# Strips of weights in passes, weight splits moved ahead, and level blocks in two alternating halves, in a two-layer hybrid block on one core

## The chip, the cores and the metric

The kernel runs on one core of one Trainium2 chip. The metric is the device time of one execution in microseconds. Three runs of the kernel before gave a median of 2342.08 us, from 2341.09 to 2344.77. The profile and the trace come from one further execution of 2344.89 us, whose span from the first to the last instruction is 2343.1 us.

## The reference

Two transformer-like blocks are applied to 512 positions (16 meta tokens are put in front, so there are 528 rows of width 1024). Everything is float32. The first block projects its normed input to retention, differential attention, a short convolution and three gates, sums the gated branches and ends with a squared-relu feed-forward. The second one has stick-breaking attention, gated linear attention (GLA) and a gated feed-forward with a convolution. What matters here, cut down:

```python
# block one
h = rms_norm(x, norm1_w)
(rq, rk, rv, rg, dq, dk, dv, cb, cc, cx, gates) = [h @ w_in[:, s:e] for s, e in column_bounds()]
ret = head_layer_norm(retention(rq, rk, rv)) * silu(rg)
diff = diff_attention(dq, dk, dv, lam, subln_w, lam_init)     # lam from four short vectors (diff_lambda)
conv = cb * short_conv(cc * cx, conv_w)
g = sigmoid(gates)
x = x + (g0 * (ret @ wb0) + g1 * (diff @ wb1) + g2 * (conv @ wb2)) @ w_out
x = x + square(relu(rms_norm(x, norm2_w) @ w_up)) @ w_down
# block two
sb = stick_breaking(q, k, v)
o = rmsnorm(gla(gq, gk, gv, glog)) * silu(g_r)                # causal, with a decay for each key channel
h = h + rmsnorm((gate_sb * (sb @ w_sb_out) + gate_gla * (o @ w_gla_out)) @ w_o)
h = h + rmsnorm((gelu(conv(hn @ w_ffn_up)) * (hn @ w_ffn_gate)) @ w_ffn_down)
```

## The kernel before

Every product with a weight matrix is cut into **strips**: 128 output columns, over up to eight chunks (`KC`) of 128 input rows. There are 338 strips, numbered through in the order of `PHASES`; two slots, even and odd numbers, hold their weights and results. To keep float32 precision, weights and inputs are split into a high and a low part, and a strip is the sum of high by high, high weight by low input, and low weight by high input. The stations of a strip:

- SyncE loads the raw weights into `wraw` (`load`), 512 KB. It waits for `lo_done` of the strip two before.
- ScalarE makes `wh` (`split_hi`, L355), when the weights have landed and the strip two before is multiplied (`mm_done`), and counts `hi_done`.
- VectorE makes `wl = wraw - wh` (`split_lo`, L857), when `hi_done` says so, and counts `lo_done`.
- TensorE multiplies (`strip`, L1548), then counts `mm_done`. The inputs are `xh`, `xl` or `bh`, `bl`. A strip over all 528 rows (T) is 48 matmuls of 264 columns, a strip over 512 positions (SEQ) is 24 of 512 columns. It waits at its start for `lo_done` of its own number and for the eviction of its slot, and with `ready` also chunk by chunk for its inputs. One chunk's three products (in steps: a step is one product of one chunk) come before the next chunk's.
- VectorE reads the result out of PSUM, mostly with the root of the norm as a factor (`scaled_by_root`, L890), and counts `evicted`.

Each engine's program is written out by hand, so the order in the code is the order in which an engine issues. `begin` (VectorE) is a `split_lo` of the next strip and a wait for the end of this one.

The **start**: ScalarE issues three small transfers (L384 to L386: `cst`, identity and ones; `col`, all columns of parameters; `lamr`, the four vectors for lambda), waits for the latter two (`params_in`, 32), and makes `xh` chunk by chunk (L363), with the `wh` of strip 0 behind the second. Behind the last come `wh` of strip 1 and the squares of x (L398). VectorE forms the lambda sums (L901), the low parts of x (L877), `wl` of strips 0 and 1, and adds up the squares (L883). TensorE sums over partitions in the middle of strip 1 (`first_sums`, L1615), and ScalarE takes the root (L379, L381). Strips 0, 1 and 2 are the first group of `conv_in`: `cc`, `cx` and `cb`; strip 2 uses slot 0.

**`gates_out`** (ScalarE) with `branch_out` (VectorE) and `branch_strips` (TensorE): for each of eight tiles a strip of gates, p0, and a strip of the branch's output matrix, p1; p2 is the next p0. The stage `sb_out` is of this kind with T-wide gates and only four chunks in p1.

**GLA** (L1933 and following): 32 iterations i, in each of which one strip is computed beside the attention of one chunk of 128 positions. `level_blocks` computes the attention inside the chunk as 64 by 64 blocks for two halves of 64 positions; each half has six levels and one diagonal product. The halves write to PSUM partitions 0 to 63 and 64 to 127 of the same bank.

## Time and profile before

| what | value |
|---|---|
| three runs | 2341.09, 2344.77, 2342.08 us (median 2342.08) |
| the profiled execution, its time | 2344.89 us |
| its span | 2343.1 us |
| TensorE busy with matmuls | 2271.0 us (97%), 13290 matmuls |
| VectorE, ScalarE, GpSimd busy | 1147.2, 780.6, 49.6 us |
| mean granted TensorE clock | 0.982 of full speed |

"Busy" counts running instructions only; waits, branches and DMA issues are not in it. Matmuls overlap, so the duration of one matmul is longer than its distance to the next; the starts of the rows are the better measure of the pace. "idle before <- releaser" in a row is how long the engine had stood still when the row began, and whose result ended that. A row that ends in x4 merges four like instructions and spans from the start of the first to the end of the last. PEclk 0.50 is the lower of the two levels of TensorE's clock, 1.2 GHz; 1.00 is 2.4 GHz.

### The profile page before, as it was taken

The page shows a single profiled execution, that of the slowest core. Times are in us where ns is not written, and L with a number is a line of the kernel's source. Part 1 is how long each engine was busy: PE and PEld are TensorE (multiplying, and loading weights), DVE is VectorE, ACT ScalarE, POOL GpSimd, SP SyncE. Part 2 cuts the span into 40 slices and gives each one's busy share as a digit, 9 for nine tenths or more (in the row PEclk, how much of TensorE's full clock was granted, in tenths as well). Part 3 has the DMA queues.
Part 4 walks back from the last instruction along what each step waited for, and adds up shares of the span by engine and source line. Part 5 has one row for each costly group of instructions (what it writes and reads, how often), then busy time and mean ns, then how long its engine had stood idle before and what let it go on. Part 6 is the DMA issues. An engine that isn't in the chain of part 4 may idle for free.

```text
span 2343.1 us, 34196 instructions
## 1 busy us (share of the span) xinstructions
PE 2271.0 (97%) x13290; PEld 1902.6 (81%) x13290; DVE 1147.2 (49%) x1726; ACT 780.6 (33%) x1207; POOL 49.6 (2%) x75
## 2 busy tenths in 40 slices
PE   7999999999999999999999999999999999999996
PEld 6988994777888788888888944789999998889895
DVE  5553322544555455454456322236765546646465
ACT  3222221322454444232234254324333324223222
POOL 0000000000000000000000000002210000000000
PEclk9999999999999999999999977999999999999999
DMA  3232220232222222222222300131113221222222
GB/s 126 90 107 90 90 81 10 72 108 81 73 68 69 101 98 95 99 91 90 100 91 88 126 1 0 63 136 64 55 55 147 90 90 64 94 94 91 99 90 99
DMA packets 53758, 197.69 MB, mean 84 GB/s; under 512 B 6928, under 2 KB 7312, under 8 KB 53024
## 3 DMA queue, kind: packets, MB, share of 16 engines
q1 hardware_dynamic: 49248, 179.39, 22.3%
q10 hardware_dynamic: 3456, 13.72, 1.6%
q0 software_dynamic: 960, 3.24, 0.5%
q8 instruction: 68, 1.11, 0.2%
q14 instruction: 26, 0.21, 0.0%
HBM read 189.91 MB, written 6.42 MB: 84 GB/s over the span
## 4 chain that ended last, share of the span: by engine, by line
PE 94%; DVE 3%; ACT 2%; issue 1%; DMA 0%; ACTq 0%; DVEq 0%
PE ps L1548 79%; PE ps L1805 1%; PE ps L1851 1%; PE ps L1930 1%; PE ps L1827 1%; PE ps L1716 1%; PE ps L1675 1%; PE ps L1744 1%; PE ps L1841 1%; DVE wl L857 1%; PE ps L1660 1%; ACT wh L355 1%; PE ps L1811 1%; PE ps L1848 0%; PE ps L1908 0%
## 5 line engine op out<-in xcount | busy, mean ns | idle before, releaser
L1548 PE MATMUL ps<-xh,wh 128*128 128x264 f32 (+1 forms) x2192 | 623.0, 333 | 28.2 <-DVE wl L857 20.3
L1548 PE MATMUL ps<-xl,wh 128*128 128x264 f32 (+1 forms) x2192 | 618.1, 331 | 0.0
L1548 PE MATMUL ps<-xh,wl 128*128 128x264 f32 (+1 forms) x2192 | 616.0, 330 | 0.0
L355 ACT ACTIVATE wh<-wraw 128x1024 fp32r<-128x1024 f32 x338 | 356.5, 1055 | 757.5 <-PE ps L1548 755.5
L857 DVE TENSOR_TENSOR wl<-wraw,wh 128x1024 fp32r<-128x1024 f32 x338 | 413.4, 1223 | 106.8 <-ACT wh L355 99.4
L1548 PE MATMUL ps<-bh,wh 128*128 128x264 f32 (+1 forms) x1600 | 448.0, 330 | 14.8 <-DVE wl L857 10.2
L1548 PE MATMUL ps<-bl,wh 128*128 128x264 f32 (+1 forms) x1600 | 445.6, 328 | 0.0
L1548 PE MATMUL ps<-bh,wl 128*128 128x264 f32 (+1 forms) x1600 | 444.2, 327 | 0.0
L1548 PEld LDWEIGHTS ps<-xh,wh 128*128 128x128 f32 x2192 | 373.5, 189 | 75.9 <-issue 19.6
L1548 PEld LDWEIGHTS ps<-xh,wl 128*128 128x128 f32 x2192 | 371.1, 190 | 37.9
L1548 PEld LDWEIGHTS ps<-xl,wh 128*128 128x128 f32 x2192 | 371.2, 189 | 37.1 <-issue 0.5
L1548 PEld LDWEIGHTS ps<-bh,wh 128*128 128x128 f32 x1600 | 268.7, 188 | 50.3 <-issue 12.6
L1548 PEld LDWEIGHTS ps<-bh,wl 128*128 128x128 f32 x1600 | 268.6, 188 | 26.7
L1548 PEld LDWEIGHTS ps<-bl,wh 128*128 128x128 f32 x1600 | 268.4, 188 | 26.7 <-issue 0.2
L890 DVE TENSOR_TENSOR gate<-ps,rsq 128x528 f32<-128x528 f32 (+1 forms) x32 | 22.4, 699 | 95.8 <-PE ps L1548 95.8
L890 DVE TENSOR_TENSOR tmp<-ps,rsq 128x528 f32<-128x528 f32 x34 | 24.1, 708 | 88.4 <-PE ps L1548 84.3
L890 DVE TENSOR_TENSOR qq<-ps,rsq 128x528 f32<-128x528 f32 (+2 forms) x36 | 25.3, 704 | 85.7 <-PE ps L1548 85.6
L363 ACT ACTIVATE bh<-hf 128x512 f32 (+1 forms) x38 | 24.0, 633 | 108.4 <-DVE hf L1495 53.7
L428 ACT ACTIVATE gate<-gate 128x512 f32<-128x512 f32 (+1 forms) x24 | 15.3, 637 | 132.2 <-DVE gate L890 132.2
L1201 DVE TENSOR_TENSOR res<-ps,res 128x512 f32 x24 | 16.6, 691 | 72.6 <-PE ps L1548 72.6
L1271 DVE SCALAR_TENSOR_TENSOR res<-ps,res 128x512 f32<-128x512 f32 (+3 forms) x32 | 17.8, 615 | 63.8 <-ACT res L666 63.8
L1218 DVE SCALAR_TENSOR_TENSOR hf<-ps,tmp 128x512 f32<-128x512 f32 x32 | 22.1, 691 | 46.0 <-ACT tmp L615 46.0
(349 smaller groups left out, 1797.8 us busy)
## 6 DMA issues: line engine op xcount, KB each, us to landing
wraw<-weights_dram SPq DMA_DIRECT2D x338, 512.0 KB, 3.2
hf<-tables_dram POOLq DMA_DIRECT2D x12, 264.0 KB, 3.0
res<-x_t_dram SPq DMA_DIRECT2D x4, 528.0 KB, 7.4
res<-x_t_dram ACTq DMA_DIRECT2D x1, 2112.0 KB, 10.6
res_dram<-res ACTq DMA_DIRECT2D x1, 2112.0 KB, 7.4
mrg_dram<-mrg ACTq DMA_DIRECT2D x1, 2112.0 KB, 11.3
mrg<-mrg_dram ACTq DMA_DIRECT2D x1, 2112.0 KB, 9.0
res<-res_dram ACTq DMA_DIRECT2D x1, 2112.0 KB, 14.9
```

The lines of the kernel that those rows point to most:

```text
L355: nc.scalar.activation(wh[:, slot], wraw[:, slot], ACT.Copy).then_inc(hi_done, 1)
L363: nc.scalar.activation(dst, src, ACT.Copy, scale=scale).then_inc(hf_hi, 1)
L857: nc.vector.tensor_tensor(wl[:, slot], wraw[:, slot], wh[:, slot].bitcast(F32), ALU.subtract)\
L890: return nc.vector.tensor_tensor(dst, src, row(rsq, n), ALU.mult)
L1548: last = nc.tensor.matmul(o, w[:, slot, c, :], a[:, c, tok], start=(c == chunks[0] and w is wh and a is hi), stop=(c == chunks[-1] and w i ...
L1660: ins = nc.tensor.matmul(o, keys, qq[:, h, NM + q0:T], start=True, stop=True)
L1675: ins = nc.tensor.matmul(o, vt[:, t, f:f + P], at[:, t - 1, q0:SEQ], start=False, stop=(t == 4))
L1716: ins = nc.tensor.matmul(ps[:, 2 + m, off:off + W], dq[h % 2][f, NM + P * b:NM + P * b + P], dk[h % 2][f, 0:W], start=True, stop=True)
L1744: ins = nc.tensor.matmul(o, vt[:, t, P * h:P * h + P], at[:, t - 1, q0:SEQ], start=False, stop=(t == 4))
L1805: nc.tensor.matmul(o, k[:, NM + P * t:NM + P * t + P], q[:, NM + P * t:T], start=(t < 3), stop=True, skip_group_check=True)
L1811: nc.tensor.matmul(ps[0:NM, z, :], k[:, 0:NM], q[:, NM:T], start=True, stop=True)
L1827: nc.tensor.matmul(o, ntri, sbt[k][:, SB0[t]:SB0[t] + L], start=False, stop=True, skip_group_check=True)
```

## The change

1. ScalarE issues `col` first, then `lamr`, then `cst`. `params_in` counts `col` alone; `lamr` has its own semaphore, and the lambda sums stand later on VectorE, behind the squares. The three small operations that finish lambda (they were L916 to L918) come after the first group of `conv_in`.
2. `split_hi` and `split_lo` of strip 2 stand ahead of the first root.
3. In `gates_out` the `split_hi` of p2 stands ahead of the wait for the gate and its sigmoid.
4. A strip without `ready` waits for `hi_done` only; it goes through all its chunks with high by high, then high weight by low input, then, after a wait for `lo_done`, low weight by high input. A strip with `ready` is as before. `first_sums` comes after step 12 of strip 1 and no longer after step 15.
5. `level_blocks` goes through the products outside and the two halves inside.

```diff
+            act.dma_start(col[:], cols).then_inc(params_in, 16)
+            act.dma_start(lamr[:], lam_rows).then_inc(lam_in, 16)
             act.dma_start(cst[:], consts).then_inc(const_in, 16)
-            act.dma_start(col[:], cols).then_inc(params_in, 16)
-            act.dma_start(lamr[:], lam_rows).then_inc(params_in, 16)
...
-            act.wait_ge(params_in, 32)
+            act.wait_ge(params_in, 16)
...
+            split_hi(*pos(START["conv_in"], 2))
             act.wait_ge(sums_done, 1)
             root(two(rsq[:, :]), ps[:, 4:6, 0:HALF], 1.0 / D)
...
                     split_hi(*p1)
+                    split_hi(*p2)
                     act.wait_ge(evicted[p0[2]], p0[1] + 1)
                     nc.scalar.activation(gate[:, T - n:T], gate[:, T - n:T], ACT.Sigmoid).then_inc(sig_done, 1)
-                    split_hi(*p2)
...
-                pe.wait_ge(lo_done, number + 1)
+                pe.wait_ge(lo_done if ready is not None else hi_done, number + 1)
...
-                for c in chunks:
-                    if ready is not None:
+                passes = ((wh, hi), (wh, lo), (wl, hi))
+                steps = [(c, *p) for c in chunks for p in passes] if ready is not None else \
+                    [(c, *p) for p in passes for c in chunks]
+                for k, (c, w, a) in enumerate(steps):
+                    if ready is None and w is wl and c == chunks[0]:
+                        pe.wait_ge(lo_done, number + 1)
+                    elif ready is not None and w is wh and a is hi:
                         pe.wait_ge(ready[0], ready[1] + c + 1)
-                    for w, a in ((wh, hi), (wh, lo), (wl, hi)):
-                        for tok, o in rows:
-                            last = nc.tensor.matmul(o, w[:, slot, c, :], a[:, c, tok],
-                                                    start=(c == chunks[0] and w is wh and a is hi),
-                                                    stop=(c == chunks[-1] and w is wl))
-                    if c in between:
-                        between[c]()
+                    for tok, o in rows:
+                        last = nc.tensor.matmul(o, w[:, slot, c, :], a[:, c, tok], start=(k == 0),
+                                                stop=(k == len(steps) - 1))
+                    if (k + 1) % 3 == 0 and k // 3 in between:
+                        between[k // 3]()
...
-                      between={4: first_sums} if k == 1 else {})
+                      between={3: first_sums} if k == 1 else {})
...
-                for g in range(2):
-                    t = slice(t0 + 64 * g, t0 + 64 * g + 64)
-                    for j in range(7):
-                        a, b = (x[1 + j],) * 2 if j < 6 else (k, q)
+                for j in range(7):
+                    a, b = (x[1 + j],) * 2 if j < 6 else (k, q)
+                    for g in range(2):
+                        t = slice(t0 + 64 * g, t0 + 64 * g + 64)
```

How instructions stand on an engine is shown at three places; a row is line, operation, output and inputs, shape, and what it waits for.

At the start, VectorE, from the low parts of x to the first product out of strip 1, before and then after:

```order
L877 SCALAR_TENSOR_TENSOR xl<-res,col,xh 128x528 [waits hf_hi] x6
L857 TENSOR_TENSOR wl<-wraw,wh 128x1024 [waits hi_done]
L883 TENSOR_TENSOR qq<-qq 128x528 [waits row_squared]
L883 TENSOR_TENSOR qq<-qq 128x528 [waits row_squared,dve_self] x6
L916 TENSOR_TENSOR small<-small 128x1 [waits lam_exps]
L917 TENSOR_SCALAR small<-small 128x1 [waits dve_self]
L918 TENSOR_SCALAR col<-col 128x1 [waits dve_self]
L890 TENSOR_TENSOR gate<-ps,rsq 128x528 [waits mm_done,root_ready,dve_self]
L931 TENSOR_TENSOR gate<-gate,rsq 128x528 [waits evicted0]
L857 TENSOR_TENSOR wl<-wraw,wh 128x1024 [waits hi_done,dve_self]
L933 TENSOR_TENSOR tmp<-ps,gate 128x528 [waits mm_done]
```

```order
L878 SCALAR_TENSOR_TENSOR xl<-res,col,xh 128x528 [waits hf_hi] x6
L858 TENSOR_TENSOR wl<-wraw,wh 128x1024 [waits hi_done]
L884 TENSOR_TENSOR qq<-qq 128x528 [waits row_squared]
L884 TENSOR_TENSOR qq<-qq 128x528 [waits row_squared,dve_self] x6
L858 TENSOR_TENSOR wl<-wraw,wh 128x1024 [waits hi_done]
L914 ISA lamr,small<-lamr 128x64 [waits lam_in]
L914 ISA small 128x1
L914 ISA lamr,small<-lamr 128x64 [waits lam_sums]
L914 ISA small 128x1
L891 TENSOR_TENSOR gate<-ps,rsq 128x528 [waits mm_done,root_ready]
L929 TENSOR_TENSOR gate<-gate,rsq 128x528 [waits evicted0]
L933 TENSOR_TENSOR tmp<-ps,gate 128x528 [waits mm_done,dve_self]
```

The third `wl`, that of strip 2, went from behind the root and two products to ahead of them.

In `sb_out`, ScalarE, one turn of the loop, before and then after:

```order
L355 ACTIVATE wh<-wraw 128x1024 [waits mm_done]
L427 REGISTER_ALU
L428 ACTIVATE gate<-gate 128x528 [waits evicted0]
L352 ISA
L354 REGISTER_ALU [waits w_loaded0]
L355 ACTIVATE wh<-wraw 128x1024 [waits mm_done]
```

```order
L355 ACTIVATE wh<-wraw 128x1024 [waits mm_done]
L352 ISA
L354 REGISTER_ALU [waits w_loaded0]
L355 ACTIVATE wh<-wraw 128x1024 [waits mm_done]
L430 ACTIVATE gate<-gate 128x528 [waits evicted0]
```

The second `wh` no longer stands behind the sigmoid, which waits for the eviction of p0.

In GLA, TensorE, a block of levels and the strip after it, before and then after (`xrows`, `res` and `qq` hold the operands of the levels and of the diagonal):

```order
L1925 MATMUL ps<-xrows 64x64
L1930 MATMUL ps<-xrows 64x64 x4
L1930 MATMUL ps<-res 64x64 x2
L1930 MATMUL ps<-qq 64x64
L1930 MATMUL ps<-xrows 64x64 x4
L1930 MATMUL ps<-res 64x64 x2
L1930 MATMUL ps<-qq 64x64
L1548 MATMUL ps<-bh,wh 128x264 [waits evicted1,lo_done,evicted0]
L1548 MATMUL ps<-bh,wh 128x264
L1548 MATMUL ps<-bl,wh 128x264 x2
L1548 MATMUL ps<-bh,wl 128x264 x2
```

```order
L1932 MATMUL ps<-xrows 64x64
L1937 MATMUL ps<-xrows 64x64 x8
L1937 MATMUL ps<-res 64x64 x4
L1937 MATMUL ps<-qq 64x64 x2
L1556 MATMUL ps<-bh,wh 128x264 [waits evicted1,hi_done,evicted0]
L1556 MATMUL ps<-bh,wh 128x264 x15
L1556 MATMUL ps<-bl,wh 128x264 x16
L1556 MATMUL ps<-bh,wl 128x264 [waits lo_done]
L1556 MATMUL ps<-bh,wl 128x264 x15
```

The halves' products now alternate, and the strip behind them waits for `hi_done` at its start and for `lo_done` before its last third.

## Rows read from the trace of the kernel before

**Rows 1.** The page, busy time, share and instructions of each engine.
```profile
PE 2271.0 (97%) x13290; PEld 1902.6 (81%) x13290; DVE 1147.2 (49%) x1726; ACT 780.6 (33%) x1207; POOL 49.6 (2%) x75
```

**Rows 2.** Waits of TensorE: waiting line, releaser, us in total, times, longest.
```profile
PE ps L1548 <- DVE wl L857: 30.5, 14, 12.6
```

**Rows 3.** Timeline of the start: start and length in us, engine, line, operation.
```profile
8.89 1.36 ACT L363 ACTIVATE xh<-res,col 128x528 fp32r<-128x528 f32 x2 [5.43 <-DMA lamr<-lam_rows_dram]
...
12.55 0.78 PE L1548 MATMUL ps<-xh,wh 128*128 128x264 f32 x2 [12.55 <-DVE wl L857]
```

**Rows 4.** DMA issues of 0.7-1.1, 1.15-1.6, 3-4 us: size, us to landing.
```profile
res<-x_t_dram SPq DMA_DIRECT2D x1, 528.0 KB, 4.7
...
wraw<-weights_dram SPq DMA_DIRECT2D x1, 512.0 KB, 5.8
...
wraw<-weights_dram SPq DMA_DIRECT2D x1, 512.0 KB, 9.0
```

**Rows 5.** Timeline around the first root, ScalarE, VectorE and TensorE.
```profile
15.80 4.36 ACT L398 ACTIVATE qq<-res 128x528 f32<-128x528 f32 x8
...
17.58 5.16 DVE L883 TENSOR_TENSOR qq<-qq 128x528 f32<-128x528 f32 x7
...
24.73 1.05 PE L1615 MATMUL ps<-qq,cst 128*128 128x264 f32 x4
...
25.82 0.70 ACT L379 ACTIVATE rsq<-ps,small 128x528 f32<-128x528 f32 x1 [5.66 <-PE ps L1615]
...
30.66 0.51 PE L1548 MATMUL ps<-xh,wh 128*128 128x512 f32 x1 [2.68 <-DVE wl L857]
```

**Rows 6.** Stretches: busy us of PE, PEld, DVE, ACT, POOL; then PEclk.
```profile
32.10:35.40 3.30, 3.30 (x9) 2.55 (x9) 3.10 (x4) 0.00 (x0) 0.00 (x0) 0.50 0.35 137
421.20:427.90 6.70, 5.84 (x14) 4.58 (x15) 4.01 (x5) 2.21 (x3) 0.00 (x0) 0.50 0.23 78
```

**Rows 7.** Timeline at the second strip of ret_gate.
```profile
419.69 1.06 ACT L355 ACTIVATE wh<-wraw 128x1024 fp32r<-128x1024 f32 x1
...
422.06 0.79 PE L1548 MATMUL ps<-xh,wh 128*128 128x512 f32 x1 [5.07 <-DVE wl L857]
```

**Rows 8.** Timeline of TensorE at the third strip of sb_qkv, the last down's second.
```profile
1284.28 0.52 PE L1548 MATMUL ps<-bh,wh 128*128 128x264 f32 x2 [0.72 <-DVE wl L857]
...
2294.17 0.50 PE L1548 MATMUL ps<-bh,wh 128*128 128x512 f32 x1 [1.08 <-DVE wl L857]
```

**Rows 9.** sb_out: waits of TensorE from 1487 to 1567; one turn on VectorE.
```profile
PE ps L1548 <- DVE wl L857: 7.2, 8, 0.9
...
1493.31 0.71 DVE L890 TENSOR_TENSOR gate<-ps,rsq 128x528 f32<-128x528 f32 x1 [3.79 <-PE ps L1548]
1495.68 1.23 DVE L857 TENSOR_TENSOR wl<-wraw,wh 128x1024 fp32r<-128x1024 f32 x1 [1.66 <-ACT wh L355]
```

**Rows 10.** Timeline of TensorE across two strip starts, 821.56 and 113.21.
```profile
821.33 0.39 PE L1548 MATMUL ps<-xh,wl 128*128 128x512 f32 x1
821.56 0.40 PE L1548 MATMUL ps<-bh,wh 128*128 128x512 f32 x1
...
112.97 0.41 PE L1548 MATMUL ps<-xh,wl 128*128 128x264 f32 x2
113.21 0.41 PE L1548 MATMUL ps<-xh,wh 128*128 128x264 f32 x2
```

**Rows 11.** The stretch of GLA, columns as in rows 6.
```profile
1610.00:1783.00 173.00, 172.86 (x1632) 162.80 (x1631) 114.79 (x198) 61.83 (x138) 33.06 (x44) 1.00 0.19 65
```

**Rows 12.** Timeline of TensorE in the first block of levels.
```profile
1618.51 0.63 PE L1930 MATMUL ps<-xrows 128*64 128x64 f32 x8
...
1619.09 0.27 PE L1930 MATMUL ps<-xrows 128*64 128x64 f32 x1
1619.15 0.22 PE L1930 MATMUL ps<-res 128*64 128x64 f32 x1
...
1619.84 0.28 PE L1930 MATMUL ps<-qq 128*64 128x64 f32 x2
```

More of the change, by code:

```diff
@@ L205, in build @@
         act_self, dve_self = sem("act_self"), sem("dve_self")
-        const_in, params_in, res_in = sem("const_in"), sem("params_in"), sem("res_in")
+        const_in, params_in, lam_in, res_in = sem("const_in"), sem("params_in"), sem("lam_in"), sem("res_in")
         x_in = [sem(f"x_in{q}") for q in range(4)]
@@ L409, in conv_strips @@
                         split_hi(*pos(B, 3 * j + 1, i, 6))
-                    split_hi(*pos(B, 3 * j + 2, i, 6))
+                        split_hi(*pos(B, 3 * j + 2, i, 6))
                     split_hi(*pos(B, 3 * j + 3, i, 6))
@@ L894, in _ @@
             nc.vector.nop().then_inc(eps_set, 1)
-            dve.wait_ge(params_in, 32)
+            dve.wait_ge(params_in, 16)
             nc.vector.tensor_tensor(wfw[:, :], wcols("final_norm_w"), wcols("norm_mix_pre_2"), ALU.mult)
-            for k in range(2):
-                if k:
-                    dve.wait_ge(lam_sums, 1)
-                a, b = lamr[:, 128 * k:128 * k + 64], lamr[:, 128 * k + 64:128 * k + 128]
-                nc.vector.tensor_tensor_reduce(out=a, in0=a, in1=b, scale=1.0, scalar=0.0, op0=ALU.mult, op1=ALU.add,
-                                               accum_out=small[:, 1 + k:2 + k]).then_inc(lam_sums, 1)
             for c in range(KC):
@@ L913, in _ @@
                 add_squares(c, slice(0, T), qq)
-            dve.wait_ge(lam_exps, 1)
-            link(nc.vector.tensor_tensor(small[:, 5:6], small[:, 4:5], small[:, 3:4], ALU.subtract))
-            link(nc.vector.tensor_scalar(small[:, 5:6], small[:, 5:6], -LAM_INIT, None, ALU.add))
-            link(nc.vector.tensor_scalar(wcol("diff_subln_w"), wcol("diff_subln_w"), 1.0 - LAM_INIT, None, ALU.mult))
+            split_lo(*pos(START["conv_in"], 2))
+            dve.wait_ge(lam_in, 16)
+            for k in range(2):
+                if k:
+                    dve.wait_ge(lam_sums, 1)
+                a, b = lamr[:, 128 * k:128 * k + 64], lamr[:, 128 * k + 64:128 * k + 128]
+                nc.vector.tensor_tensor_reduce(out=a, in0=a, in1=b, scale=1.0, scalar=0.0, op0=ALU.mult, op1=ALU.add,
+                                               accum_out=small[:, 1 + k:2 + k]).then_inc(lam_sums, 1)
             B = START["conv_in"]
@@ L925, in conv_strips @@
                     p = [pos(B, 3 * j + k, i, 6) for k in range(4)]
-                    if not (isinstance(i, int) and j == 0):
+                    first = isinstance(i, int) and j == 0
+                    if not first:
                         split_lo(*p[1])
@@ L931, in conv_strips @@
                     link(nc.vector.tensor_tensor(gate[:, :], gate[:, :], rsq[:, :], ALU.mult))
-                    begin(p[1], p[2])
+                    if not first:
+                        split_lo(*p[2])
+                    dve.wait_ge(mm_done, p[1][0] + 1)
                     nc.vector.tensor_tensor(two(tmp[:, j]), slot_ap(p[1][2], T), two(gate[:, :]), ALU.mult)\
@@ L948, in _ @@
             conv_strips(0)
+            dve.wait_ge(lam_exps, 1)
+            link(nc.vector.tensor_tensor(small[:, 5:6], small[:, 4:5], small[:, 3:4], ALU.subtract))
+            link(nc.vector.tensor_scalar(small[:, 5:6], small[:, 5:6], -LAM_INIT, None, ALU.add))
+            link(nc.vector.tensor_scalar(wcol("diff_subln_w"), wcol("diff_subln_w"), 1.0 - LAM_INIT, None, ALU.mult))
             with link.loop(1, KC // 2, 2 * 5) as i:
```

## The prediction, made before the changed kernel ran

> **What bounds the kernel now.** I read the page first: TensorE is busy for 2271.0 us, 97% of the span [rows 1]. No other engine comes near, so a change pays only by what it takes off TensorE's own time line: idle stretches, a lower clock, or matmuls that could run side by side. Next I read the list of TensorE's waits. Its largest entry is `DVE wl L857`, the low part of a strip's weights, 30.5 us in 14 waits [rows 2]. I then looked for each of the 14 in the timeline: the start (12.55), the third strip (2.68), `ret_gate` (5.07), `ret_out` (1.1), `sb_qkv` (0.72), `sb_out` (eight, 7.2) and the last `glu` down (1.08) make up the 30.5. Last I read the granted clock of the stretches behind them. The profiled execution took 2344.89 us, 2.8 above the median of 2342.08; I take the sum off the span and carry the same difference over to the median.
>
> **Part 1, the start.** `params_in` now counts `col` alone, and `col` goes out first on ScalarE's queue. Before, ScalarE's first operation waited to 8.89 for `lamr`; from there to the first matmul at 12.55 are 3.66 us [rows 3]: two `xh` (1.36), `wh` (1.06 [rows 7]), `wl` (1.23 [rows 9]). The first x tiles, issued between 0.7 and 1.1, were there 4.7 later at about 5.4, and strip 0's weights, issued in the half microsecond after that, at 7.0 [rows 4]. So the two `xh` run at 5.5 to 6.9, `wh` from 7.05 (now the weights are the last to come), `wl` to 9.4, first matmul at 9.45: **3.1 us** earlier. `cst`, which TensorE waits for too, becomes the last transfer of its queue; the last one, `lamr`, landed at 8.8 before [rows 3], 0.6 us ahead of the need. Strip 0 still waits chunk by chunk; all of x lands ahead of strip 1's weights, which share its queue (12.5, below), and the last chunk is wanted at 14.6 at the earliest. The 3.1 is between 2.0 (weights or `cst` a microsecond later) and 3.6.
>
> **Part 2, the third strip.** Strip 1 ended at about 28.0, and strip 2 waited 2.68 us to 30.66: its `wh` stood behind the root on ScalarE (25.82), its `wl` behind that and two products on VectorE [rows 5]. After the change the split stands ahead of the root. By then: strip 1's weights land at 3.5 + 9.0 = 12.5 [rows 4], `wh` of strip 1 ends at 13.8, the eight squares (4.36) at 18.1, `wh` of strip 2 at 19.2; VectorE's adds (5.16, from 15.0) end at 20.2, and `wl` of strip 2 and the `lam` sums, 1.23 + 0.5 more, at 22.0. TensorE comes to the column sums three steps of 0.24 and 3.1 us earlier than at 24.73, at 20.9, 0.7 behind the adds. From the start of the sums to the root 1.1, two operations of 0.7 for the root and 0.7 for the eviction of strip 0 make 3.2, against the sums' own 0.9 and 2.9 for the twelve steps of strip 1 that are left: strip 2 starts with no wait. That is 2.7. The clock too: right after that gap it was 1.2 GHz from 32.1 to 35.4 [rows 6], where a 512-column matmul lasted 0.63 instead of 0.40; half of 3.4 us, 1.7, goes with the gap. **4.4 us.** What is late next there is the eviction of strip 0, with 0.6 to spare. Between 2.7 (the clock falls anyway) and 4.4.
>
> **Part 3, strips that wait for `wh` alone.** A strip without `ready` makes all its high-by-high products first and needs `wl` only at two thirds, 3.7 to 3.9 us in. VectorE's 1.2 us is then hidden behind sixteen steps of TensorE. This matters only where TensorE stood still:
> - Second strip of `ret_gate`: idle 5.07 us to 422.06, while `wh` was ready at 420.75 [rows 7]. **1.3 us.** The table load and the root ahead of it stay, 3.8 us of idling, and a fall of the clock to 1.2 GHz with them (421.2 to 427.9 [rows 6], 3.1 us lost). I leave the fall as it was, the nearest rows being gaps of 2.68 and 5.07, which both had one behind them; without it 3.1 more, if it covers busy time alone 0.3 less.
> - Third strip of `sb_qkv`: 0.72 idle: **0.7**. Second strip of the last `glu` down: 1.08 idle: **1.1** [rows 8]. Both waits are shorter than the 1.23 of `wl`, so `wh` was there before the idling began.
> - A first strip with `ready`, as `ret_out`'s second (its wait of 1.1), keeps its wait for `wl`: nothing.
> - Everywhere else `wl` came in time even for the strip's start, and VectorE's order there is the same, so the added wait in mid-strip finds it done. The wait itself I cost at nothing: at strip starts, where waits stand too (821.56, 113.21), the next matmul follows at the same 0.23, or 0.24 for two short ones, as inside a strip [rows 10].
>
> **Part 4, `gates_out`.** In `sb_out` the second strip has only four chunks (3.06 us), too little for VectorE's `gate` (from 1493.31), the sigmoid, `wh` and `wl` (from 1495.68) in a row. Eight waits, 7.2 us [rows 9]. The slot of `wh` was free as soon as `gate` could start, since both wait for the same strip. With the split ahead of the sigmoid `wh` ends 1.1 us after the strip ahead, 2 us before it is wanted; `wl` is hidden as in part 3. The sigmoid comes 0.4 later, but its product waits for the strip, 3.06. **7.2 us**; at least 5, if something that I do not see takes 0.3 each time. In `conv_out` and `ret_out` (5.6 us strips) nothing was idle and nothing is gained. Queued behind the moved split on ScalarE is the sigmoid alone. The SP queue's loads hang on `lo_done`, which comes no later.
>
> **Part 5, the level blocks.** From 1610 to 1783 TensorE is busy 172.86 of 173.00 us [rows 11]; what shortens its work there is paid out in full, since VectorE's chain for the next head runs from the end of one block to the start of the next. A block is 28 records on L1930, 14 for each half (an fp32 matmul leaves two), each 0.058 after the one before: 1618.51 to 1619.90. The rows show the halves side by side for a moment: a `xrows` of the second half starts at 1619.09, before the `res` (1619.15) and `qq` of the first [rows 12]. Three overlap so; eleven of the second half do not. In the new order a half's neighbour is always the other half's, so 11 x 0.058 = 0.64 less one trailing pair, 0.58 a block; 16 blocks: **9.3 us**, between 0 (no overlap beyond what was there) and 10.2. I take the upper part, as the rows show overlap over three instructions, and pairs need only two.
> The Trainium skill says otherwise in "TensorE: Matmul & The Clock Gate", Part 3, under what overlaps and what doesn't: weight loads overlap running matmuls only when the row groups differ, and matmuls start in order. Both halves use all rows; by that rule this part would be worth 0. The row at 1619.09 speaks against it, as a later matmul with its own weights started ahead of an earlier one.
>
> **The sum.** 3.1 + 4.4 + 1.3 + 0.7 + 1.1 + 7.2 + 9.3 = 27.1 us. From the profiled run 2344.89 - 27.1 = 2317.8; from the median 2342.08 - 27.1 = **2315.0**.
>
> **Rivals.**
> - *The halves do not overlap further.* For: only three instructions are seen to do so, perhaps the most that can. Against: while they do, each half keeps its 0.058. 2315.0 + 9.3 = 2324.3. Chance 0.13. This is also the result of the rule cited.
> - *The clock does not fall behind the shorter gap of part 3.* 3.1 less: 2311.9. Chance 0.12.
> - *The start or the third strip is bound elsewhere*: `cst` last on its queue, or the evictions of strip 0. For: margins of 0.6 us only. Up to 2 + 2 us back: 2319. Chance 0.10.
> - *The change doesn't do what it says in `sb_out`*: the gap stays, with another releaser. 2322.2. Chance 0.05. Against: every link of the chain is in the rows.
> - *Slower: pass by pass makes the matmuls themselves slower.* Now each one reads another chunk of `xh` and other weights than its neighbour, while before the same weights served high and low. 3 x (2192 + 1600) = 11376 matmuls come 0.23 (512 columns) or 0.12 (264) after one another [rows 10]. The rows give pitches to 0.01, and those between two with the same weights are no shorter than those where weights change, which speaks against it. But 5 ns each would be 57 us, 2372; it decides from (27.1 + 4.7) / 11376 = 2.8 ns. Chance 0.04. A nanosecond either way, 11 us, is inside what I can't exclude; I take 5 us of it into the range.
>
> **How the numbers follow.** The forecast has a chance of 0.56, the rivals the rest. The range runs from 2315.0 less 3.1 and 5, 2307, to the halves' rival with a little of the start, 2326; outside it are the slower rival and some of the pitch. Under 0.2% (4.7 us) a measurement of this kernel can't tell from no change. Faster needs 4.7 of 27.1 us: all cases but the slower one and losses of several parts at once give it, 0.93; within 0.2% 0.04; slower 0.03.
>
> **What would show it.** First matmul near 9.5, no idle before strip 2, no 1.2 GHz stretch near 30. In `sb_out` no wait of TensorE for `wl`, eight pairs of strips in 9.05 us each instead of 9.97. A block of L1930 in 0.8 us and not 1.4. Idle before `ret_gate`'s second strip 3.8. Pitches of 0.23 and 0.12 as before. Wrong would be: a new releaser on TensorE's list with more than 5 us, L1930 as long as before, or a busy TensorE beyond 2262 us, which would be slower matmuls.

## The result and the profile after

The changed kernel took 2303.42 us (median of five runs, 2297.68 to 2305.23); the kernel before, on the same chip, 2342.08. The ratio is 0.9828, with a 95% interval from 0.9816 to 0.9839. That is faster, as forecast, but 38.7 us and not 27.1: 2303.4 lies outside the predicted range of 2307 to 2326. The profiled execution took 2305.12 us, its span is 2303.3.

The page's busy times against [rows 1], then the list of TensorE's waits (waiting line, releaser, us in total, times, longest) against [rows 2]:

```profile
PE 2247.8 (98%) x13290; PEld 1883.9 (82%) x13290; DVE 1148.9 (50%) x1726; ACT 781.1 (34%) x1207; POOL 49.5 (2%) x75
```

```profile
PE ps L1556 <- DMA cst<-consts_dram: 9.0, 1, 9.0
...
PE ps L1556 <- ACT wh L355: 3.8, 1, 3.8
...
PE ps L1556 <- DVE wl L858: 1.1, 1, 1.1
```

Of the 30.5 us that TensorE waited for `wl`, 1.1 are left (`ret_out`); 9.0 at the start now end with `cst`, 3.8 at `ret_gate` with `wh`. But TensorE is also *busy* for 23.2 us less, with the same 13290 matmuls. The prediction had 9.3 us of such a gain for the level blocks and 1.7 by the clock. Most of the rest has to be in the pace of ordinary matmuls, the distance from one start to the next.

The timeline of the start (start and length in us, engine, line, operation), as in [rows 3]: ScalarE's first operation comes at 5.13 and not 8.89, `wl` ends at 8.86, and the first matmul comes at 8.96 and not 12.55.

```profile
5.13 1.36 ACT L363 ACTIVATE xh<-res,col 128x528 fp32r<-128x528 f32 x2 [1.68 <-DMA col<-cols_dram]
...
6.54 1.06 ACT L355 ACTIVATE wh<-wraw 128x1024 fp32r<-128x1024 f32 x1
7.63 1.23 DVE L858 TENSOR_TENSOR wl<-wraw,wh 128x1024 fp32r<-128x1024 f32 x1 [0.28 <-ACT wh L355]
...
8.96 0.80 PE L1556 MATMUL ps<-xh,wh 128*128 128x264 f32 x2 [8.96 <-DMA cst<-consts_dram]
```

In TensorE's timeline strip 2 follows strip 1 with no idle time (against 30.66 [2.68] in [rows 5]); `ret_gate`'s second strip waits 3.81 us for `wh` (against 5.07 in [rows 7]):

```profile
22.15 2.10 PE L1556 MATMUL ps<-xh,wl 128*128 128x264 f32 x16
...
24.08 2.03 PE L1556 MATMUL ps<-xh,wh 128*128 128x512 f32 x8
...
410.16 2.23 PE L1556 MATMUL ps<-xh,wh 128*128 128x512 f32 x5 [3.81 <-ACT wh L355]
```

TensorE's timeline in the first block of levels, as in [rows 12]. From the product that joins the halves (L1932) to the strip behind the block it is 1.07 us; before it was 1.71 (from 1618.34 to 1620.05):

```profile
1593.40 0.27 PE L1932 MATMUL ps<-xrows 128*64 128x64 f32 x1
1593.41 0.27 PE L1937 MATMUL ps<-xrows 128*64 128x64 f32 x1
...
1593.52 0.62 PE L1937 MATMUL ps<-xrows 128*64 128x64 f32 x14
...
1594.26 0.28 PE L1937 MATMUL ps<-qq 128*64 128x64 f32 x3
1594.47 0.76 PE L1556 MATMUL ps<-bh,wh 128*128 128x264 f32 x4
```

And what the prediction had put at nothing: stretches without a wait, in which TensorE runs 264-column strips only, first before (`ret_qkv`; `gla_gates`, `gla_proj` and `w_o`), then after. The columns are busy us of PE with the count of matmuls, PEclk, DMA share, GB/s:

```profile
250.00:300.00 50.00, 50.00 (x411) 1.00 0.26 89
1795.00:1915.00 120.00, 120.00 (x983) 1.00 0.26 88
```

```profile
240.00:290.00 50.00, 50.00 (x416) 1.00 0.27 90
1760.00:1880.00 120.00, 120.00 (x994) 1.00 0.27 92
```

Both are at full clock, both fully busy; in 120 us there are 994 matmuls and not 983, which is 1.1% more. From the starts of all 6600 intervals between 264-column matmuls of one strip (those at 2.4 GHz) the mean is 122.17 ns before and 120.88 ns after; for 512 columns it is 231.9 and 231.8. 1.30 ns x 6600 = **8.6 us**.

### The profile page after: what moved, and what is told of

Its sections match the earlier page's. It is cut to its first block, busy times and chain, and to the rows that moved or that the text cites. A ratio compares the mean times of both kernels' runs of the same rounds, so it can differ in the third digit from the quotient of the medians.

```text
span 2303.3 us, 34172 instructions
## 1 busy us (share of the span) xinstructions
PE 2247.8 (98%) x13290; PEld 1883.9 (82%) x13290; DVE 1148.9 (50%) x1726; ACT 781.1 (34%) x1207; POOL 49.5 (2%) x75
## 4 chain that ended last, share of the span: by engine, by line
PE 96%; DVE 2%; ACT 1%; issue 0%; DMA 0%; ACTq 0%; DVEq 0%
PE ps L1556 81%; PE ps L1812 1%; PE ps L1858 1%; PE ps L1834 1%; PE ps L1723 1%; PE ps L1682 1%; PE ps L1751 1%; PE ps L1848 1%; PE ps L1667 1%; PE ps L1937 1%; PE ps L1818 1%; PE ps L1855 0%; PE ps L1915 0%; PE ps L1763 0%; PE ps L1680 0%; PE ps L1749 0%
## 5 line engine op out<-in xcount | busy, mean ns | idle before, releaser
L1556 PE MATMUL ps<-xh,wh 128*128 128x264 f32 (+1 forms) x2192 | 412.8, 332 | 20.7 <-DMA cst<-consts_dram 9.0
L1556 PE MATMUL ps<-xl,wh 128*128 128x264 f32 (+1 forms) x2192 | 405.3, 329 | 0.0
L1556 PE MATMUL ps<-xh,wl 128*128 128x264 f32 (+1 forms) x2192 | 404.4, 329 | 0.0
L1556 PEld LDWEIGHTS ps<-xh,wh 128*128 128x128 f32 x2192 | 332.5, 189 | 64.0 <-DMA cst<-consts_dram 8.9
L1556 PEld LDWEIGHTS ps<-xl,wh 128*128 128x128 f32 x2192 | 332.9, 189 | 38.9
L1556 PEld LDWEIGHTS ps<-xh,wl 128*128 128x128 f32 x2192 | 332.3, 189 | 38.6
L1556 PE MATMUL ps<-bh,wh 128*128 128x264 f32 (+1 forms) x1600 | 299.8, 330 | 5.7 <-DVE xl L1295 1.8
L1556 PE MATMUL ps<-bl,wh 128*128 128x264 f32 (+1 forms) x1600 | 296.3, 328 | 0.0
L1556 PE MATMUL ps<-bh,wl 128*128 128x264 f32 (+1 forms) x1600 | 295.1, 327 | 0.0
L1556 PEld LDWEIGHTS ps<-bh,wl 128*128 128x128 f32 x1600 | 240.0, 188 | 27.3
```

What stands on the lines that cost most here:

```text
L1556: last = nc.tensor.matmul(o, w[:, slot, c, :], a[:, c, tok], start=(k == 0), stop=(k == len(steps) - 1))
```

## The experiments

Ratios are to the kernel before on the same chip, with their 95% intervals. Executions of one kernel differ by up to 12 us, and their profiles by how many stretches at 1.2 GHz they have, most of them in the stick-breaking attention (67 to 90 us in a whole profile; 88 before, 86 after), so a part is judged by its own rows first and by the time second. "Pace" is the mean distance of the starts inside strips, at full clock.

**The order alone.** The strip's loop of the changed kernel in the kernel before, with the wait for `lo_done` left at the strip's start:

```diff
-                for c in chunks:
+                passes = ((wh, hi), (wh, lo), (wl, hi))
+                steps = [(c, *p) for c in chunks for p in passes] if ready is not None else \
+                    [(c, *p) for p in passes for c in chunks]
```

> The kernel before, with the order of the products alone changed: pass by pass in a strip without ready, but the wait for lo_done stays at the strip's start; nothing of the other parts. Theory A (the order itself makes 264-column matmuls follow one another faster): their mean pitch goes from 0.1222 to 0.1209 us, over some 6600 intervals 8.5 us, so 2333.5 us, TensorE's idle time as before. Theory B (the extra gain of the changed kernel came from elsewhere, the clock or the shorter waits, as the prediction priced the order at nothing): 2342 within 0.2%, pitch 0.1222. The rival of the prediction (slower matmuls) would give more than 2342.

Measured: 2336.97 us, ratio 0.9964 (0.9952 to 0.9977), a gain of between 5.4 and 11.2 us. The pace is 120.88 ns. The stretches (columns as above) hold as many matmuls as in the changed kernel, while the timeline shows strip 2's gap as long as before:

```profile
248.00:298.00 50.00, 50.00 (x416) 1.00 0.28 90
1780.00:1900.00 120.00, 120.00 (x994) 1.00 0.30 104
```

```profile
30.45 2.98 PE L1550 MATMUL ps<-xh,wh 128*128 128x512 f32 x8 [2.70 <-DVE wl L857]
```

Theory A holds: the order of the products by itself makes them faster. The reverse, the changed kernel with the order chunk by chunk:

```diff
-                pe.wait_ge(lo_done if ready is not None else hi_done, number + 1)
+                pe.wait_ge(lo_done, number + 1)
...
+                for c in chunks:
+                    if ready is not None:
+                        pe.wait_ge(ready[0], ready[1] + c + 1)
+                    for w, a in ((wh, hi), (wh, lo), (wl, hi)):
```

> The changed kernel with chunk by chunk order put back in every strip (and so with the wait for lo_done at the strip's start and the column sums after step 15); start, third strip, gates_out and level blocks as changed. Theory A: 8.5 us come back by the pitch, and 1.3 + 1.3 of ret_gate and the last glu down; sb_out keeps its gain only as far as wl is in time: wh now ends 2 us before the need and wl 1.2 behind it, so no gap, or a few tenths a turn. About 2303.4 + 11 = 2314.5. Theory B: only the 2.6 us of the waits come back, 2306, with T strips still 5.67 us from the first start to the last.

Measured: 2319.41 us, ratio 0.9888 (0.9870 to 0.9906), pace 122.16 ns; the same two stages hold as few matmuls as before. The time is 5 us over the forecast 2314.5, with executions from 2311 to 2323, so the pace is what this run shows, and not the time:

```profile
240.00:290.00 50.00, 50.00 (x411) 1.00 0.25 84
1765.00:1885.00 120.00, 120.00 (x983) 1.00 0.28 91
```

From 1470 to 1560 (`sb_out`) its TensorE has no wait for `wl` in the list: the eight gaps are gone without the pass order.

**The other parts, one at a time.** The level blocks alone, the loops of `level_blocks` swapped in the kernel before:

> The kernel before, with the two halves of the level blocks alternating, nothing else. By the trace of the changed kernel, from the start of the product that joins the halves to the last of the block is 0.64 us shorter: 16 x 0.64 = 10.2 us, 2331.9. The prediction's 9.3 would give 2332.8; the rule that matmuls on the same rows don't overlap would give 2342.1. If a part of the 10.2 needs the other changes (the strip that follows has a wait less), it is less than 9.

Measured: 2334.39 us, ratio 0.9966 (0.9953 to 0.9978). In TensorE's timeline its first block takes 1.08 us from the joining product to the strip, as in the changed kernel:

```profile
1615.46 0.27 PE L1925 MATMUL ps<-xrows 128*64 128x64 f32 x1
...
1615.58 0.62 PE L1930 MATMUL ps<-xrows 128*64 128x64 f32 x14
...
1616.54 0.51 PE L1548 MATMUL ps<-bh,wh 128*128 128x264 f32 x2
```

Summed over the starts of all sixteen blocks that is 10.2 us, so the part stands by itself. The split in `gates_out` alone, in the kernel before:

```diff
                     split_hi(*p1)
+                    split_hi(*p2)
                     act.wait_ge(evicted[p0[2]], p0[1] + 1)
                     nc.scalar.activation(gate[:, T - n:T], gate[:, T - n:T], ACT.Sigmoid).then_inc(sig_done, 1)
-                    split_hi(*p2)
```

> The kernel before with the split of the next gates strip ahead of the gates' sigmoid, nothing else; the order chunk by chunk and the wait for lo_done at the start stay. In the run with chunk order put back into the changed kernel the eight gaps of sb_out were gone without the pass order, so here they go too. If a gap is worth its idle time: 7.2 us, 2335. If it is worth the distance of the two starts less a normal step, as the comparison of the two traces says: 1.10 each and not 0.9, 8.8 us, 2333.3. If the pass order is needed: under 3 us.

Measured: 2335.62 us, ratio 0.9960 (0.9946 to 0.9973). TensorE's waits for `wl` are 7.0 us shorter than in [rows 2]; the eight distances between the last matmul of p1 and the first of p2 are 8.5 us shorter. The remaining two parts were undone one by one in the changed kernel. The third strip's splits, behind the root again:

```diff
-            split_hi(*pos(START["conv_in"], 2))
             act.wait_ge(sums_done, 1)
...
-                        split_hi(*pos(B, 3 * j + 2, i, 6))
+                    split_hi(*pos(B, 3 * j + 2, i, 6))
```

(and the same on VectorE.)

> The changed kernel with the splits of the third strip behind the first root again, on ScalarE and VectorE. The prediction's term is 2.7 for the gap and 1.7 for the 1.2 GHz stretch; with pass order the third strip needs only wh at its start, so the gap that comes back is shorter than 2.68 by the 1.23 of wl: 1.5, or 1.7 by the starts, and the stretch of 3.4 us at 1.2 GHz comes back if a gap so short is enough for it (1.7). Forecast 2303.4 + 3.4 = 2306.8; without the stretch 2305.1. If the gap doesn't come back at all, the pass order alone would have removed it, and the term belongs to that part.

Measured: 2310.30 us, ratio 0.9857 (0.9828 to 0.9886), an interval that reaches the changed kernel's. By its timeline the gap did not come back, nor the stretch at 1.2 GHz, and strip 3 (the fourth) starts at 29.32, in the changed kernel at 29.65:

```profile
19.84 1.16 PE L1619 MATMUL ps<-qq,cst 128*128 128x264 f32 x4 [0.31 <-DVE qq L883]
...
22.41 1.04 ACT L355 ACTIVATE wh<-wraw 128x1024 fp32r<-128x1024 f32 x1
...
23.75 0.64 PE L1553 MATMUL ps<-xh,wh 128*128 128x512 f32 x2
...
29.32 2.10 PE L1553 MATMUL ps<-xh,wh 128*128 128x264 f32 x16
```

The miss is instructive. `wh` behind the root is ready at 23.45, 0.3 ahead of TensorE's 23.75: with sums at step 12 and a strip that needs only `wh` at its start, the third strip has no gap even with its splits where they were. In the run with the order chunk by chunk, which has the splits moved, the third strip started 0.52 us behind the pair of matmuls ahead, 0.3 more than a normal step. So each of the two moves is enough by itself, but for those 0.3. That strip 3 starts no later is partly the clock's doing: it rose 3.1 us after the first matmul here and 5.6 us after it in the changed kernel, so strip 1 starts at 16.43 and not at 17.40. From there to strip 3 it is 12.9 us and not 12.3, with 0.31 us of waiting for the squares ahead of the column sums. The 7 us between the medians are in no row of this stretch; its profiled execution, at 2307.38 us, has 68 us at 1.2 GHz in the stick-breaking attention, and the changed kernel's 54.

Then the small transfers in their old order:

```diff
+            act.dma_start(cst[:], consts).then_inc(const_in, 16)
             act.dma_start(col[:], cols).then_inc(params_in, 16)
             act.dma_start(lamr[:], lam_rows).then_inc(lam_in, 16)
-            act.dma_start(cst[:], consts).then_inc(const_in, 16)
...
             act.wait_ge(params_in, 16)
+            act.wait_ge(lam_in, 16)
```

> The changed kernel with the three small transfers in their old order and ScalarE's first operation waiting for lamr again. First matmul at about 12.5 and not at 9.17; everything behind it 3.4 us later: 2306.8. If the third strip or the sums swallow part of it (they depend on ScalarE too), less.

Measured: 2308.27 us, ratio 0.9858 (0.9836 to 0.9880).

```profile
12.60 0.78 PE L1557 MATMUL ps<-xh,wh 128*128 128x264 f32 x2 [12.60 <-DVE wl L859]
```

The first matmul is 3.6 us later, strip 3 only 2.7: in this profile TensorE's clock rose 3.4 us after the first matmul, in the changed kernel's 5.6 us after it.

**What in the order does it.** First the sequence of products: column halves outside the chunks; weights kept and inputs changed in the first sixteen steps; inputs kept and weights changed.

```diff
-                    [(c, *p) for p in passes for c in chunks]
+                    [(c, *p, r) for p in passes for r in rows for c in chunks]
```

> The changed kernel; within a pass the two column halves of a T strip are outside and the chunks inside, so that PSUM's bank changes twice a pass and not with each matmul, and every matmul has other weights than the one before. If the pitch is set by what a matmul reads after what (the same weights twice or not, bank after bank), the mean moves from 0.1209 in either direction: the two halves sharing weights is what makes it fast: back to 0.122 or more, 2312; alternating banks is what costs: under 0.120, 2297 or less. If only the repetition of an order through the chunks counts, 0.1209 and 2303.4 stay.

```diff
-                    [(c, *p) for p in passes for c in chunks]
+                    [(c, *p) for c in chunks for p in passes[:2]] + [(c, *passes[2]) for c in chunks]
```

> The changed kernel, but a strip without ready first takes both products with the high weights chunk by chunk (high input, low input), and then the low weights with the high input for all chunks. Weight tiles follow one another as in the pass order, the input tile changes at every step of the first sixteen. From the runs before: 264-column matmuls follow one another at 0.1222 us chunk by chunk, at 0.1209 pass by pass, at 0.1223 pass by pass with the column halves outside. Theory M (a change of the input tile costs): 0.1217 here, 4 to 6 us over the changed kernel's time. Theory W (a change of the weight tile costs): 0.1209, no difference. Theory S (only a steady walk through the chunks by pairs is fast): 0.1222 in the first two thirds, 0.1209 in the last, the same 0.1217; then same_input gives as much.

```diff
-                    [(c, *p) for p in passes for c in chunks]
+                    [(c, *p) for c in chunks for p in (passes[0], passes[2])] + [(c, *passes[1]) for c in chunks]
```

> The changed kernel, but a strip without ready first takes high and low weights with the same high input chunk by chunk, and then the high weights with the low input for all chunks (so it waits for lo_done at its start, and ret_gate and the last glu down lose 2.6 us again). The weight tile changes at every step of the first sixteen, the input tile never. Theory M: pitch 0.1209, 2306. Theory W: 0.1217, 2311. Theory S: 0.1217, 2311.

| kernel | median us | ratio (interval) | pace, 264 columns | pace, 512 columns |
|---|---|---|---|---|
| halves outside (rows_outer) | 2312.33 | 0.9854 (0.9841 to 0.9867) | 122.32 ns | 231.8 ns |
| weights kept (two_groups) | 2307.09 | 0.9843 (0.9828 to 0.9858) | 121.54 ns | 232.0 ns |
| input kept (same_input) | 2313.29 | 0.9869 (0.9854 to 0.9884) | 121.55 ns | 231.9 ns |

With the halves outside, the pace is as slow as chunk by chunk, though each pass still goes up through the chunks. That run parts the two halves that share a weight, changes how often the PSUM bank alternates and changes the walk through the input, all at once, so it can't say which of the three costs; its expectation gave the shared weights for this outcome.

The last two agree to 0.01 ns in the mean, and interval by interval to 1 ns, so theories M and W fall and S stays: it makes no difference whether the weight tile or the input tile changes, only that a chunk is taken in two steps running. (Much of the 6 us between their times comes from the wait for `lo_done` at the strip's start: same_input has 5.07 us of idling at `ret_gate` again and 6.8 us at 1.2 GHz there, two_groups 3.81 and 3.4.) Next, then, the walk itself and the addresses under it, all in the kernel best1 (below; pace 120.89 and 231.8):

(`walk` then stands for `chunks` in the passes; the cuts show the line that differs.)

```diff
+                walk = [*chunks][0::2] + [*chunks][1::2]
```

> The kernel best1 (2297.0 us) with another walk through the chunks in each pass: 0, 2, 4, 6, 1, 3, 5, 7. The two kernels whose first sixteen steps take each chunk twice in a row had the same intervals whichever tile, weights or input, was changed, 0.1215 on average; so it is the sequence of chunks that counts. Theory D (the distance from one chunk to the next sets the pitch): the mean of the 264-column matmuls moves off 0.1209 by half a nanosecond or more, either way, 3 us or more in time. Theory N (only that a pass never takes the same chunk in two steps running): 0.1209 and 2297 stay.

```diff
+                walk = [*chunks][::-1]
```

> The kernel best1 with the chunks of each pass walked downwards, 7 to 0. Theory D (the distance counts, and so perhaps its sign): off 0.1209. Theory N: 0.1209, 2297.

```diff
-        xh, xl = sb("xh", [P, KC, T], F32R), sb("xl", [P, KC, T], F32R)
+        xh, xl = (sb(t, [P, KC, T + 16], F32R)[:, :, 0:T] for t in ("xh", "xl"))
```

> The kernel best1 (2297.0 us) with the chunks of xh and xl 544 columns apart and not 528, bh and bl as they were: same instructions, same order, other addresses. Theory A (the addresses that follow one another set the pitch, so the order works through them): the 264-column matmuls of the x strips move off 0.1209 us, those of the b strips stay; time off 2297 by up to 8 us either way. Theory B (the order works through the instructions, not the addresses): x and b strips both keep 0.1209 and the pattern 121, 120, 122, 121, 116, 119, 122, 126 ns; 2297.

The same with 8 columns for all four tiles:

> The kernel best1 with the chunks of xh, xl, bh and bl 536 columns apart and not 528. Theory A: both kinds of strips move off 0.1209, and by another amount than with 544. Theory B: 0.1209, 2297.

```diff
+        sb("gap", [P, 16])
         wraw = sb("wraw", [P, 2, KC, P])
```

> The kernel best1 with the weights (wraw, wh, wl) and what lies behind them 64 bytes further on; inputs and strides as before. Theory A1 (it is the relation of a weight's address to an input's that counts): the pitch moves. Theory A2 (only the walk within a tile counts, its stride): 0.1209 stays here though it moves with the strides. Theory B: nothing moves.

| kernel | median us | ratio (interval) | 264 columns, from xh, xl, ns | from bh, bl | 512 columns |
|---|---|---|---|---|---|
| best1 | 2296.99 | 0.9797 (0.9784 to 0.9811) | 120.8 | 121.0 | 231.8 |
| evens, then odds | 2305.75 | 0.9839 (0.9821 to 0.9857) | 122.0 | 121.9 | 232.0 |
| downwards | 2301.88 | 0.9822 (0.9801 to 0.9844) | 121.0 | 121.0 | 233.6 |
| xh, xl at 544 | 2301.57 | 0.9817 (0.9801 to 0.9834) | 122.5 | 121.0 | 231.4 |
| all at 536 | 2312.93 | 0.9865 (0.9839 to 0.9890) | 122.6 | 122.3 | 232.4 |
| weights 64 bytes on | 2296.69 | 0.9796 (0.9778 to 0.9813) | 120.8 | 120.9 | 231.8 |

The run with 544 columns carries its own control, as its timeline of TensorE shows. Its passes over `bh` and `bl` start 1.93 us apart, those over `xh` and `xl` 1.96, sixteen matmuls each, the same instructions in the same execution a few us later:

```profile
1788.86 2.10 PE L1573 MATMUL ps<-bh,wh 128*128 128x264 f32 x16
1790.79 2.10 PE L1573 MATMUL ps<-bl,wh 128*128 128x264 f32 x16
...
1800.54 2.12 PE L1573 MATMUL ps<-xh,wh 128*128 128x264 f32 x16
1802.50 2.12 PE L1573 MATMUL ps<-xl,wh 128*128 128x264 f32 x16
```

and in `ret_qkv`, x strips only, 410 matmuls stand in the 50 us in which best1 and the changed kernel have 416:

```profile
240.00:290.00 50.00, 50.00 (x410) 1.00 0.26 84
```

So the addresses at which the input is read one after the other set the pace: theory D for the walk (`best_evens`), theory A for the stride.

By its mean, the run with the weights moved looks as if it did not matter where they lie (theory A2). Its single intervals say otherwise. In best1 a pass over a 264-column strip goes 121, 120, 122, 121, 116, 119, 123, 126 ns and then over again (medians over the strips). With the weights 64 bytes on it goes 123, 126, 121, 120, 122, 121, 116, 119: the same eight, two places or one chunk later. Five of the six kinds of pass do so, one of them from its third interval on; the sixth, which opens a strip over `xh`, is less regular. The inputs had not moved; what lies behind the weights had, but no strip reads it. So where the weights lie against the inputs takes part in setting each interval (theory A1), and the walk at this stride goes through the whole sequence wherever it begins, so that its mean stays. Whether moved weights would change the mean with another stride no run shows.

**A faster kernel.** Three more moves like those of the change:

```diff
+                    if h == RH:
+                        split_hi(*pos(START["ret_gate"], 1))
                     act.wait_ge(sq_used, n_sq)
                     root(qq[:, w, NM:T], ps[:, 2 * (w % 2) + 1, :], 1.0 / RDV)
...
                     split_hi(*p1)
+                    if isinstance(i, int):
+                        table_set(SIGMOID)
                     split_hi(*p2)
...
             def first_sums():
+                pe.wait_ge(const_in, 16)
```

> The changed kernel and three more moves of the same kind: the splits of ret_gate's second strip ahead of the last root (ScalarE and VectorE), the first split of gates_out ahead of the load of the sigmoid's table, and TensorE's wait for cst at the first column sums and not at its start. Theory: ret_gate's idle 3.81 and the 1.2 GHz stretch of 3.4 us behind it go (3.8 + 0.2 + 1.7 = 5.7 us), ret_out's 1.12 goes (1.2), the first matmul starts at 8.95 with wl and not at 9.17 (0.2): 2303.4 - 7.1 = 2296.3. Rival: the clock falls anyway (2298), or the second strip's end is then held up by wl or by the eviction of the first strip, and the idle time moves one strip on (2300 to 2303).

Measured: 2296.99 us (2295.97 to 2297.61), ratio 0.9797 (0.9784 to 0.9811): 0.3% below the changed kernel, the intervals don't meet. From the start of the first gate strip to that of the second it is 7.3 us and not 11.65, so 4.4 us shorter. (Measured from further ahead it would be 6.0, but 1.7 of that is a stretch at 1.2 GHz near 340 that the changed kernel's profile has and this one doesn't, in the attention, where none of the moves is.) In the timeline the first matmul now waits for `wl`, and an idle time is left at 411.14; the stretch behind the second gate strip's start is at full clock:

```profile
8.93 0.81 PE L1573 MATMUL ps<-xh,wh 128*128 128x264 f32 x2 [8.93 <-DVE wl L867]
...
411.14 1.19 PE L1573 MATMUL ps<-xh,wh 128*128 128x512 f32 x4 [1.00 <-ACT wh L355]
```

```profile
403.90:407.30 3.40, 3.40 (x15) 1.00 0.13 54
```

The rival was right in a small way: 1.00 us of idle time turned up one strip on, where `wh` stands behind the first silu and its product. From the second gate strip's start to `ret_out`'s first strip the two kernels take the same 40.6 us: what the clock gave back there, the new gap took. What else the rows show of the gain is the 1.1 us wait at `ret_out`, which is gone from the list.

## Why the prediction was wrong, step by step

The shares of the change, from the distances between starts in the two traces. A gap's worth is the distance across it less a normal step.

| step | predicted | measured |
|---|---|---|
| 1, start | 3.1 | 3.6 |
| 2, third strip: gap and clock | 2.7 + 1.7 | 2.8 + 1.7 |
| 3, `ret_gate`: gap and clock | 1.3 + 0 | 1.3 + 1.3 |
| 3, `sb_qkv`, last `glu` down | 0.7 + 1.1 | 0.9 + 1.25 |
| 4, `sb_out` | 7.2 | 8.5 |
| 5, level blocks | 9.3 | 10.2 |
| pace of the 264-column matmuls | 0 | 8.6 |
| sum | 27.1 | 40.2 (the spans differ by 39.8) |

**The step that failed** is the last of the part by part working, put into the rival "pass by pass makes the matmuls themselves slower": the pace was taken as unchanged. Its evidence was [rows 10], that distances between two matmuls with the same weights are no shorter than those where weights change. That is so, and it says nothing on the walk through the inputs, which is what the order changed. The rows also give starts to 0.01 us only, and 1.3 ns is far below that; the text knew that a nanosecond is worth 11 us, and yet gave it 5 us of the range. With 8.6 for that term the working comes to 2315.0 - 8.6 = 2306.4. The remaining 3 us are in the smaller terms below.

**Part 1** was right in mechanism. It is 0.5 better since strip 0's weights, which it had landing last, at 7.0, were there by 6.54, when `wh` began. `cst` is the last to come (9.0), as feared, but only a tenth behind `wl` (8.86): waited for later, in best1, it gave 0.03 us. A new releaser with over 5 us was one of the prediction's signs of being wrong; here it was a false alarm.

**Part 2** has the right size under the wrong owner. All of it came, 4.5 us, but late_third shows that strips that start on `wh` and sums three steps earlier bring it without the moved splits. The prediction priced the parts one after the other and didn't ask whether one made another needless.

**Part 3.** The idle time at `ret_gate` fell from 5.07 to 3.81, as forecast, and the stretch at 1.2 GHz behind it, which the prediction left as long as it was, lasted 3.4 us and not the 6.8 of [rows 6] (columns as above):

```profile
410.70:414.10 3.40, 3.40 (x9) 0.53 0.43 153
```

From the second gate strip's start to `ret_out`'s first the changed kernel is 1.3 us shorter by that. The rival that the clock would not fall at all was half right: with 3.81 us of idling ahead it fell for half as long, in all five profiles with that gap (the changed kernel, late_third, old_start, rows_outer, two_groups), and in best1, with none ahead of this strip, not at all. With 5.07 us ahead it stayed down for 6.8 us in five profiles of six, but for only 3.4 in after_chunks, so part of the 1.3 can be luck.

**Part 4** was right: the gaps in `sb_out` went, and a pair of strips takes 8.70 us, as TensorE's timeline shows, where 9.05 was forecast. Of the 0.35 more 0.17 is the gap, sized by its idle time, and 0.09 the pace (72 x 1.3 ns); the other 0.1 is the first step behind the gap, where in the kernel before the second matmul starts 0.22 us after the first and not 0.12.

```profile
1478.42 1.13 PE L1556 MATMUL ps<-xh,wh 128*128 128x264 f32 x8
...
1487.12 1.13 PE L1556 MATMUL ps<-xh,wh 128*128 128x264 f32 x8
```

The step behind the gap, in TensorE's timeline of the kernel before: the pair at 1497.04 is followed 0.34 later, other pairs 0.24 later.

```profile
1497.04 0.50 PE L1548 MATMUL ps<-bh,wh 128*128 128x264 f32 x2 [0.93 <-DVE wl L857]
1497.38 0.40 PE L1548 MATMUL ps<-bl,wh 128*128 128x264 f32 x2
1497.62 0.40 PE L1548 MATMUL ps<-bh,wl 128*128 128x264 f32 x2
```

A gap of 0.9 us idle is worth 8.5 / 8 = 1.07, since the row of the last matmul ahead of it ends 0.28 after its start, where the next would have started 0.12 after it. Gaps that vanish whole were priced 0.1 to 0.2 too low by their idle time (0.72 idle was worth 0.88, 1.08 was worth 1.25), and each costs about 0.1 more in the step behind it, which the table's 8.5 leaves out.

**Part 5** was right. The blocks are 0.64 us shorter, 0.58 was forecast, and levels_only shows the gain by itself. The Trainium skill's rule in "TensorE: Matmul & The Clock Gate", Part 3, that weight loads overlap only with other row groups, read by itself as the prediction read it, would have given 0; the trace does not agree for these 64-column products in two column halves, whose starts come 4 ns apart in pairs. The prediction took one sentence for the whole: the same Part 3 also has matmuls in distinct column groups run side by side, as these do.

## What to carry to other kernels

Where matmuls are most of the time, the pace has to be counted over hundreds of them, before and after a change of order, of a tile's stride or of the walk through its parts: 1% that no single row shows was worth more here than any one gap. Price a gap from start to start, not by its idle time. And where two parts of a change hide the same wait, ask for each what it is worth with the other in place.

## What the runs showed of the hardware that was not expected

- The addresses at which inputs are read set the pace of float32 matmuls in the strips. 264-column ones followed one another in 120.8 to 122.6 ns, 512-column ones in 231.4 to 233.6, by the stride of the chunks (528, 536, 544 columns of 4 bytes) and the walk (up, down, evens first, each chunk twice). The two kinds don't agree on the best: downwards is nearly as good for 264 columns and worst for 512; 544 is bad for 264 and slightly better for 512. Moving the weights by 64 bytes left the means as they were, but shifted the sequence of the single intervals by one chunk, so the weights' addresses count too. Why an address sequence is fast stays open. The intervals repeat after four chunks in the fast case; with the other walks and strides they don't repeat within the eight chunks of a pass.
- Two float32 products in different column halves, in turns, start nearly in pairs (4 and 54 ns apart), though both use all rows.
- After the first matmul TensorE's clock stayed at 1.2 GHz for between 3.0 and 6.0 us in these profiles. The difference moves all that follows by up to 1.5 us, half of the 3.0, whatever was changed at the start.
- Behind an idle time of 2.7 us at the third strip the clock fell for 3.4 us in all four profiles that had it, behind 3.81 us at `ret_gate` for 3.4, and behind the 1.0 us in best1 and its five variants not at all.
